# Layer norm behind the sliding-window attention: who centres, how many passes VectorE makes, and where the bias is added

## The chip, the cores and the metric

One core of one Trainium2 chip. The metric is device time in microseconds (us) of one execution. A NeuronCore has TensorE (PE in the profile; PEld is its weight load), VectorE (DVE), ScalarE (ACT), GpSimd (POOL) and SyncE (SP, which here only issues DMAs).

## The reference, cut to what matters

The program is two transformer-like blocks over 256 tokens of width 1024, all in float32. The change touches one norm of the second block, behind its sliding-window attention (index 1 of `ln_mix`):

```
for i in range(2):
    mix = ssd_shortconv_layer_mixer(x, ...) if i == 0 else sliding_window_attention(x, ...)
    x = layer_norm(ALPHA * x + mix, ln_mix_g[i], ln_mix_b[i])      # (x - mean) * rsqrt(var + 1e-5) * g + b
    x = layer_norm(ALPHA * x + (silu(x @ w_gate[i]) * (x @ w_up[i])) @ w_down[i], ln_ffn_g[i], ln_ffn_b[i])
    x = x + (p[i] @ w_ple[i]) * sigmoid(x @ w_ple_gate[i] + b_ple_gate[i])
```

So the norm's result is used twice: as the operand of the gate and up projections (11 chunks of 256 columns each), and, ALPHA times, as the residual of the next norm.

## The kernel before

**Products.** Each float32 product is made of three float32r matmuls: high part by high part, high by low, low by high. Weights come in units of at most 512 KB: SP loads a unit into one of 5 slots of `raw`, ScalarE copies it into one of 6 slots of `whi` (rounded, the high half; `high_halves(until)` does so up to a unit number), GpSimd makes `wlo = raw - whi`. SP refills a raw slot when its low half is made (`w_lo`), ScalarE refills a `whi` slot when TensorE is done with it (`w_used`). The order in which ScalarE does splits, turns and everything else is written out by hand; each engine runs its instructions in that order.

**Activations.** The operand of a product lies turned (features in partitions) in `XThi` and `XTlo` (two halves of `XT`). The stream lies in `X`, two tiles `t` of 128 tokens by 1024. To turn a half `h` (512 features) of a tile, TensorE makes four 128x128 transposes into a bank of PSUM (`turn_half`, helper line L1954), ScalarE copies the bank into `XThi` (`turn_tile`), and VectorE writes bank minus high part into `XTlo` (`turn_half`, L1129). Counters: `xh` (a half of `X` is normed), `t_pe`, `t_hi`, `t_lo`. TensorE's first feed-forward chunk `fg1_0` waits for `t_lo`: its first four rows of k want two halves of low parts (lower features of both tiles, by VectorE's order), its last four want all.

**The norm** (`layer_norm_by_tile`, name `x7`). The attention's output product is `ao0` and `ao1` (512 columns each); its last matmuls are L2675 to L2677. For each tile: VectorE adds the product to the scaled stream into a PSUM bank (`residual`, L1712), takes statistics of both halves (`bn_stats`, L1902, L1913, L1718), and their aggregate (L1719); ScalarE makes rsqrt as exp(-0.5 ln) (`layer_norm`); VectorE refines it by a Newton step (`refine_columns`, L1150 to L1156). Then VectorE makes two passes for each half: `centred`, (x - mean) * g in place (L1724), and `scaled`, times r plus b, into `X` (L1730). The rows g and b are held as `lnr[:, 0]` and `lnr[:, 1]`, broadcast over partitions.

**Around it.** TensorE's order: six `pw1_0` matmuls of tile 0 (L1982 to L1984, the product with `p`), turn of tile 0's first half, `pw1_1` of tile 0, turn of tile 0's second half, `pw1_0` and `pw1_1` of tile 1, the two turns of tile 1, feed-forward (L2016 high, L2023 low). ScalarE's: splits, root of tile 0, three splits, root of tile 1, turn of tile 0, copy of `pw1_0` to `pwt`, turn of tile 1, a split, copy of `pw1_1`. Columns such as conv weights are loaded as rows (`ROWS_B`), turned once near the start, and read by `bcol(name, j)`.

Of the kernel before, what the change touches and what calls it, by code (L numbers as in the profile page):

```python
# [211 lines left out]
ROWS_B = (("ssd_conv_w", 48), ("ssd_conv_b", 12), ("sc_conv_w", 24), ("ssd_norm_w", 8), ("b_qk", 10))  # L212
# [13 lines left out]
def build(nc, a, out):  # L226
# [8 lines left out]
    with ctx:  # L235
# [204 lines left out]
        def head_part(t, j):  # L440
# [15 lines left out]
            ln_in ln_sum ln_rs xh h_x h_g h_hi h_lo a_kd g_x g_s x_end t_half x7_t x7_f q_in act_seq dve_seq out_done""".split()  # L456
# [21 lines left out]
        def landed(name):  # L478

            return chunks[name][2]  # L480
# [118 lines left out]
        def _(act):  # L599
# [7 lines left out]
            def fn(out_, in_, func, **k):  # L607
                return nc.scalar.activation(out_, in_, func, **k)  # L608
# [42 lines left out]

            def turn_tile(name, hi, t):

                g0 = turns[name][0]
                for h in range(2):
                    g = g0 + 2 * t + h
                    act.wait_ge(S["t_pe"], g + 1)
                    bank = pm[:, g % 4, :].rearrange("p (f t) -> p f t", t=P)
                    fn(hi[:, 4 * h:4 * h + 4, t * P:(t + 1) * P], bank, ACT.Copy).then_inc(S["t_hi"], 1)
# [334 lines left out]

            def feed_forward(i):
# [4 lines left out]
                high_halves(mixed + SPLIT)  # L1000
                layer_norm(2 * i, 1)
                turn_tile(("x4", "x7")[i], XThi, 0)
                leave(f"pw{i}_0", pwt[:, 0])
                turn_tile(("x4", "x7")[i], XThi, 1)
                leave(f"pw{i}_1", pwt[:, 1])
# [91 lines left out]
        def _(v):  # L1097
# [25 lines left out]
            def turn_half(name, hi, lo, t, h):  # L1123
# [5 lines left out]
                V.tensor_tensor(lo[:, part[0], part[1]], bank, hi[:, part[0], part[1]].bitcast(F32),  # L1129
                                ALU.subtract).then_inc(S["t_lo"], 1)  # L1130
# [15 lines left out]
            def refine_columns(first, n):  # L1146
# [5 lines left out]
                for c in cols:  # L1152
                    last = V.tensor_scalar(rw[:, c], rw[:, c], -0.5, 1.5, ALU.mult, ALU.add)
# [631 lines left out]
            def feed_forward(i):  # L1785
                for c in range(DFF2 // HW):
# [9 lines left out]
                    if k:  # L1796
# [10 lines left out]
                                    ALU.subtract).then_inc(S["h_lo"], 1)  # L1807
                layer_norm(2 * i + 1, 2, (f"fd{i}_0", f"fd{i}_1"), ("x5", "x8")[i])
# [88 lines left out]
            def layer_norm_by_tile():  # L1897

                v.wait_ge(S["x7_t"], 1)
# [6 lines left out]
                summed(2, "x7", 0)  # L1906
                first_half(2, 0, "x7", 0)
                link(centred(2, 0, "x7", 0, 1))
# [860 lines left out]
```

## Time and profile before

| | us |
|---|---|
| median of 3 runs | 1247.16 (1245.83, 1247.16, 1247.21) |
| the profiled execution | 1247.44 |
| its span | 1245.6 |
| TensorE busy | 1231.2 (99%) |
| VectorE, ScalarE, GpSimd busy | 494.5, 658.1, 943.3 |
| mean granted clock of TensorE | 0.998 of full |

Busy time is the sum over one engine's instructions. TensorE's busy share says how little it waits, not how fast it works. The span is that of the instructions; 1.8 us of the execution lie around it. All times of rows below are from the start of the span.

### The profile page before, as it was taken

What the parts mean: (1) busy time and instruction counts of PE and PEld (TensorE: products, weight loads), DVE (VectorE), ACT (ScalarE), POOL (GpSimd) and SP (SyncE); (2) the same over time, 40 slices, a digit from 0 to 9 for tenths busy, and PEclk for the clock granted to TensorE, in tenths of its full rate; (3) what the DMA queues carried; (4) which work ended last, traced back from release to release, by engine and by line L of the source; (5) the groups of instructions that cost most, each with busy time, mean ns of one, the idle gap of its engine ahead of it and who ended that gap; (6) DMA issues with size and microseconds to landing.
All of it is one profiled execution on the core that took longest, in us unless ns stands there. A gap on an engine that the chain in (4) does not pass through costs nothing.

```text
span 1245.6 us, 18466 instructions
## 1 busy us (share of the span) xinstructions
PE 1231.2 (99%) x7505; PEld 1067.9 (86%) x7505; DVE 494.5 (40%) x899; ACT 658.1 (53%) x878; POOL 943.3 (76%) x409
## 2 busy tenths in 40 slices
PE   8999999999999999999999999999999999999998
PEld 7988888888888888899899888888879877888886
DVE  6635334551234310047652153342053674334025
ACT  6773656656466653345544464444445655444433
POOL 7865357838969898866589788889867657888974
PEclk9999999999999999999999999999999999999999
DMA  9754236625746666654466766666638445666651
GB/s 302 205 148 142 72 111 185 179 92 171 219 148 206 186 203 202 192 157 120 136 187 203 246 202 187 187 189 198 202 120 287 140 122 164 188 186 186 208 163 68
DMA packets 147757, 218.31 MB, mean 175 GB/s; under 512 B 9387, under 2 KB 79578, under 8 KB 147674
## 3 DMA queue, kind: packets, MB, share of 16 engines
q1 hardware_dynamic: 144282, 209.92, 55.5%
q10 hardware_dynamic: 3392, 7.23, 1.6%
q8 instruction: 59, 0.97, 0.3%
q14 instruction: 24, 0.20, 0.1%
HBM read 216.07 MB, written 1.05 MB: 174 GB/s over the span
## 4 chain that ended last, share of the span: by engine, by line
PE 93%; DVE 3%; ACT 2%; DMA 1%; POOL 1%; issue 1%; POOLq 0%; ACTq 0%; DVEq 0%
PE acc L2016 18%; PE acc L2053 12%; PE acc L2055 12%; PE acc L2054 12%; PE acc L2023 9%; PE pm L2069 6%; PE acc L2060 4%; PE acc L2062 4%; PE acc L2063 4%; PE acc L1982 1%; PE acc L1983 1%; PE acc L1984 1%; ACT whi L608 1%; PE acc L2263 1%; PE pm L1944 1%; POOL wlo L594 1%
## 5 line engine op out<-in xcount | busy, mean ns | idle before, releaser
L594 POOL TENSOR_TENSOR wlo<-raw,whi 128x1024 fp32r<-128x1024 f32 (+4 forms) x404 | 942.5, 2357 | 290.3 <-ACT whi L608 288.0
L608 ACT ACTIVATE whi<-raw 128x1024 fp32r<-128x1024 f32 (+4 forms) x404 | 410.7, 1035 | 274.8 <-PE acc L2055 134.5
L2016 PE MATMUL acc<-XT,whi 128*128 128x512 f32 x960 | 231.2, 393 | 0.0
L2016 PEld LDWEIGHTS acc<-XT,whi 128*128 128x128 f32 x960 | 177.5, 189 | 34.8 <-issue 0.2
L2023 PEld LDWEIGHTS acc<-XT,wlo 128*128 128x128 f32 x960 | 123.4, 191 | 4.8
L2023 PE MATMUL acc<-XT,wlo 128*128 128x256 f32 x960 | 124.8, 283 | 0.0
L2060 PE MATMUL acc<-XT,whi 128*128 128x256 f32 x432 | 123.2, 285 | 1.4 <-DVE XT L1118 1.4
L2053 PE MATMUL acc<-whi,XT 128*128 128x512 f32 (+4 forms) x320 | 122.7, 383 | 0.1
L2062 PE MATMUL acc<-XT,whi 128*128 128x256 f32 x432 | 122.2, 283 | 0.0
L2063 PE MATMUL acc<-XT,wlo 128*128 128x256 f32 x432 | 122.2, 283 | 0.0
L2054 PE MATMUL acc<-wlo,XT 128*128 128x512 f32 (+4 forms) x320 | 119.4, 373 | 0.0
L2055 PE MATMUL acc<-whi,XT 128*128 128x512 f32 (+4 forms) x320 | 119.4, 373 | 0.0
L2060 PEld LDWEIGHTS acc<-XT,whi 128*128 128x128 f32 x432 | 82.8, 192 | 2.3 <-issue 2.1
L2062 PEld LDWEIGHTS acc<-XT,whi 128*128 128x128 f32 x432 | 82.9, 192 | 0.1
L2063 PEld LDWEIGHTS acc<-XT,wlo 128*128 128x128 f32 x432 | 82.8, 192 | 0.0
L2053 PEld LDWEIGHTS acc<-whi,XT 128*128 128x128 f32 x320 | 60.1, 188 | 11.4 <-issue 1.3
L2055 PEld LDWEIGHTS acc<-whi,XT 128*128 128x128 f32 x320 | 60.1, 188 | 10.0
L2054 PEld LDWEIGHTS acc<-wlo,XT 128*128 128x128 f32 x320 | 60.2, 188 | 9.3 <-issue 0.2
L1712 DVE SCALAR_TENSOR_TENSOR pm<-X,acc 128x512 f32<-128x512 f32 x16 | 10.8, 692 | 108.9 <-PE acc L2055 63.7
L2053 PE MATMUL acc<-whi,Hhi 128*128 128x512 f32 x136 | 52.9, 389 | 0.0
L2054 PE MATMUL acc<-wlo,Hhi 128*128 128x512 f32 x136 | 52.9, 389 | 0.0
L2055 PE MATMUL acc<-whi,Hlo 128*128 128x512 f32 x136 | 52.9, 389 | 0.0
(423 smaller groups left out, 1952.4 us busy)
## 6 DMA issues: line engine op xcount, KB each, us to landing
raw<-in_w_in SPq DMA_DIRECT2D x68, 512.0 KB, 3.9
raw<-in_w_ff SPq DMA_DIRECT2D x64, 512.0 KB, 3.8
raw<-in_w_gate SPq DMA_DIRECT2D x44, 512.0 KB, 3.7
raw<-in_w_up SPq DMA_DIRECT2D x44, 512.0 KB, 3.8
raw<-in_w_down SPq DMA_DIRECT2D x44, 512.0 KB, 4.2
raw<-in_w_in_mix SPq DMA_DIRECT2D x36, 512.0 KB, 3.8
raw<-in_w_branch SPq DMA_DIRECT2D x16, 512.0 KB, 3.7
raw<-in_w_out_mix SPq DMA_DIRECT2D x16, 512.0 KB, 3.3
```

The costliest lines, as they stand in the source:

```text
L594: nc.gpsimd.tensor_tensor(piece(wlo, u), piece(raw, u), piece(whi, u).bitcast(F32), ALU.subtract).then_inc(S["w_lo"], 1)
L608: return nc.scalar.activation(out_, in_, func, **k)
L1944: last = T.transpose(pm[:, (g0 + g) % 4, f * TOK + t * P:f * TOK + (t + 1) * P], src[:, t, k * P:(k + 1) * P], ident)
L2016: T.matmul(acc[:, n % 2, f, :], piece(whi, u)[:, i, f * P:(f + 1) * P], XT[:, :, k, :], start=k == 0, stop=False)
L2023: last = T.matmul(acc[:, n % 2, f, 0:TOK], piece(wlo, u)[:, i, f * P:(f + 1) * P], XThi[:, k, :], start=False, stop=k == kt - 1)
L2053: T.matmul(o, hi[:, k, tok], wh, start=opens, stop=False)
L2054: T.matmul(o, hi[:, k, tok], wl, start=False, stop=False)
L2055: last = T.matmul(o, lo[:, k, tok], wh, start=False, stop=done)
L2060: T.matmul(o, wh[:, fs], hi[:, k, :], start=opens and f % 2 == 0, stop=False, skip_group_check=True)
L2062: T.matmul(o, wh[:, fs], lo[:, k, :], start=False, stop=False, skip_group_check=True)
L2063: last = T.matmul(o, wl[:, fs], hi[:, k, :], start=False, stop=done, skip_group_check=True)
L2069: return T.matmul(o, lhs, rhs, start=start, stop=stop, **k)
```

## The change

ScalarE centres the norm's rows in PSUM (`centre`: -x + mean, with the mean as a pointer bias). `refine_columns` gives the root a negative sign, and VectorE makes one pass for each half (`unbiased`: times the root, times g, into `X`). The bias b is added in two places: as a column, when the turned operand leaves PSUM (ScalarE's and VectorE's copies of a half become four 128x128 pieces each, since the column differs by 128 features), and to the stream `X` by two VectorE sums of 128x1024 inside the feed-forward, behind chunks 1 and 2. TensorE's order has `pw1_0` of tile 1 ahead of the first turn. ScalarE's order: centring of tile 0 behind its root, one split instead of three, copy of `pw1_0`, turn of tile 0's first half, root and centring of tile 1, the other turned halves, then the two splits that are left and the copy of `pw1_1`. VectorE takes tile 1's first residual ahead of tile 0's root.

```diff
@@ -209,7 +209,7 @@
           ("dn_conv_w", 48), ("norm2_g", 8), ("sg_v_norm_g", 4))
-ROWS_B = (("ssd_conv_w", 48), ("ssd_conv_b", 12), ("sc_conv_w", 24), ("ssd_norm_w", 8), ("b_qk", 10))
+ROWS_B = (("ssd_conv_w", 48), ("ssd_conv_b", 12), ("sc_conv_w", 24), ("ssd_norm_w", 8), ("b_qk", 10), ("ln_mix_b", 8))
...
@@ -649,14 +649,22 @@
+            def turn_half(name, hi, t, h, bias=None):
+                g = turns[name][0] + 2 * t + h
+                act.wait_ge(S["t_pe"], g + 1)
+                bank = pm[:, g % 4, :].rearrange("p (f t) -> p f t", t=P)
+                if bias is None:
+                    last = fn(hi[:, 4 * h:4 * h + 4, t * P:(t + 1) * P], bank, ACT.Copy)
+                else:
+                    for f in range(4):
+                        last = fn(hi[:, 4 * h + f, t * P:(t + 1) * P], bank[:, f, :], ACT.Identity, bias=bias(4 * h + f))
+                last.then_inc(S["t_hi"], 1)
             def turn_tile(name, hi, t):
-                g0 = turns[name][0]
-                for h in range(2):
-                    g = g0 + 2 * t + h
-                    act.wait_ge(S["t_pe"], g + 1)
-                    bank = pm[:, g % 4, :].rearrange("p (f t) -> p f t", t=P)
-                    fn(hi[:, 4 * h:4 * h + 4, t * P:(t + 1) * P], bank, ACT.Copy).then_inc(S["t_hi"], 1)
+                turn_half(name, hi, t, 0)
+                turn_half(name, hi, t, 1)
...
@@ -992,17 +1000,39 @@
+            def centre(t):
+                for c in range(2):
+                    x = pm[:, (turns["x7"][0] + 2 * t + c) % 4, :]
+                    fn(x, x, ACT.Identity, scale=-1.0, bias=moments[:, t, 0:1]).then_inc(S["x7_c"], 1)
             def feed_forward(i):
                 mixed = landed(("mo1b", "ao1c")[i])
                 high_halves(mixed - (APART, 3)[i] + SPLIT)
                 logs()
                 layer_norm(2 * i, 0)
-                high_halves(mixed + SPLIT)
-                layer_norm(2 * i, 1)
-                turn_tile(("x4", "x7")[i], XThi, 0)
-                leave(f"pw{i}_0", pwt[:, 0])
-                turn_tile(("x4", "x7")[i], XThi, 1)
-                leave(f"pw{i}_1", pwt[:, 1])
+                if i == 0:
+                    high_halves(mixed + SPLIT)
+                    layer_norm(0, 1)
+                    turn_tile("x4", XThi, 0)
+                    leave("pw0_0", pwt[:, 0])
+                    turn_tile("x4", XThi, 1)
+                    leave("pw0_1", pwt[:, 1])
+                else:
+                    def bias(f):
+                        return bcol("ln_mix_b", f)
+                    centre(0)
+                    high_halves(mixed - 2 + SPLIT)
+                    act.wait_ge(S["w_used"], landed("pw1_0"))
+                    fn(pwt[:, 0], accT("pw1_0"), ACT.Copy).then_inc(evac_at("pw1_0")[0], 1)
+                    turn_half("x7", XThi, 0, 0, bias)
+                    layer_norm(2, 1)
+                    centre(1)
+                    turn_half("x7", XThi, 0, 1, bias)
+                    turn_half("x7", XThi, 1, 0, bias)
+                    turn_half("x7", XThi, 1, 1, bias)
+                    high_halves(mixed + SPLIT)
+                    leave("pw1_1", pwt[:, 1])
                 for c in range(DFF2 // HW):
...
@@ -1120,14 +1150,22 @@
-            def turn_half(name, hi, lo, t, h):
+            def turn_half(name, hi, lo, t, h, bias=None):
                 g = turns[name][0] + 2 * t + h
                 v.wait_ge(S["t_hi"], g + 1)
                 bank = pm[:, g % 4, :].rearrange("p (f t) -> p f t", t=P)
                 part = slice(4 * h, 4 * h + 4), slice(t * P, (t + 1) * P)
-                V.tensor_tensor(lo[:, part[0], part[1]], bank, hi[:, part[0], part[1]].bitcast(F32),
-                                ALU.subtract).then_inc(S["t_lo"], 1)
+                if bias is None:
+                    last = V.tensor_tensor(lo[:, part[0], part[1]], bank, hi[:, part[0], part[1]].bitcast(F32),
+                                           ALU.subtract)
+                else:
+                    for f in range(4):
+                        last = V.scalar_tensor_tensor(out=lo[:, 4 * h + f, part[1]], in0=bank[:, f, :],
+                                                      scalar=bias(4 * h + f),
+                                                      in1=hi[:, 4 * h + f, part[1]].bitcast(F32),
+                                                      op0=ALU.add, op1=ALU.subtract)
+                last.then_inc(S["t_lo"], 1)
...
@@ -1143,14 +1181,14 @@
-            def refine_columns(first, n):
+            def refine_columns(first, n, sign=1.0):
                 cols = [slice(c, c + 1) for c in range(first, first + n)]
                 for c in cols:
                     last = V.tensor_scalar(rw[:, c], rv[:, c], rs[:, c], rs[:, c], ALU.mult, ALU.mult)
                 link(last)
                 for c in cols:
-                    last = V.tensor_scalar(rw[:, c], rw[:, c], -0.5, 1.5, ALU.mult, ALU.add)
+                    last = V.tensor_scalar(rw[:, c], rw[:, c], -0.5 * sign, 1.5 * sign, ALU.mult, ALU.add)
                 link(last)
...
@@ -1805,6 +1843,8 @@
                                     ALU.subtract).then_inc(S["h_lo"], 1)
+                    if i == 1 and c in (1, 2):
+                        link(V.tensor_tensor(X[:, c - 1, :], X[:, c - 1, :], lnr[:, 1, :], ALU.add))
                 layer_norm(2 * i + 1, 2, (f"fd{i}_0", f"fd{i}_1"), ("x5", "x8")[i])
...
@@ -1896,6 +1936,27 @@
+                def moments_of(t):
+                    summed(2, "x7", t)
+                    v.wait_ge(S["ln_sum"], 2 * 2 + t + 1)
+                    link(variance(rv[:, t:t + 1], moments[:, t, 1:2], 1, 1e-5))
+                def root(t):
+                    v.wait_ge(S["ln_rs"], 2 * 2 + t + 1)
+                    refine_columns(t, 1, -1.0)
+                def unbiased(t, c):
+                    cols = slice(c * W, (c + 1) * W)
+                    v.wait_ge(S["x7_c"], 2 * t + c + 1)
+                    V.scalar_tensor_tensor(out=X[:, t, cols], in0=staged("x7", t, c), scalar=rs[:, t:t + 1],
+                                           in1=lnr[:, 0, cols], op0=ALU.mult, op1=ALU.mult).then_inc(S["xh"], 1)
+                def bias(f):
+                    return bcol("ln_mix_b", f)
                 v.wait_ge(S["x7_t"], 1)
...
@@ -1903,25 +1964,26 @@
                 v.wait_ge(S["x7_f"], 2)
-                summed(2, "x7", 0)
-                first_half(2, 0, "x7", 0)
-                link(centred(2, 0, "x7", 0, 1))
-                scaled(0, "x7", 0, 1)
+                moments_of(0)
                 v.wait_ge(S["w_used"], landed("ao0c"))
                 residual(2, "ao0c", "x7", 0, 1).then_inc(evac_at("ao0c")[0], 1)
+                root(0)
+                v.wait_ge(S["ln_in"], 16 * 5 * 2)
+                unbiased(0, 0)
+                unbiased(0, 1)
                 v.wait_ge(*evac_at("ao0c"))
                 V.bn_stats(stats[:, 1, 0, :], staged("x7", 1, 0))
                 v.wait_ge(S["w_used"], landed("ao1c"))
                 residual(2, "ao1c", "x7", 1, 1).then_inc(evac_at("ao1c")[0], 1)
                 v.wait_ge(*evac_at("ao1c"))
-                summed(2, "x7", 1)
-                first_half(2, 0, "x7", 1)
-                turn_half("x7", XThi, XTlo, 0, 0)
-                link(centred(2, 0, "x7", 1, 1))
-                scaled(0, "x7", 1, 1)
-                turn_half("x7", XThi, XTlo, 1, 0)
-                turn_half("x7", XThi, XTlo, 0, 1)
-                turn_half("x7", XThi, XTlo, 1, 1)
+                moments_of(1)
+                turn_half("x7", XThi, XTlo, 0, 0, bias)
+                root(1)
+                unbiased(1, 0)
+                unbiased(1, 1)
+                turn_half("x7", XThi, XTlo, 1, 0, bias)
+                turn_half("x7", XThi, XTlo, 0, 1, bias)
+                turn_half("x7", XThi, XTlo, 1, 1, bias)
...
@@ -2691,13 +2753,13 @@
             unit_T("pw1_0", begun("pw1_0", 0), PThi, PTlo, 0)
+            enter("pw1_0")
+            unit_T("pw1_0", begun("pw1_0", 0), PThi, PTlo, 1).then_inc(S["w_used"], 1)
             turn_half("x7", 2, 0, 0)
             pe.wait_ge(S["w_lo"], begun("pw1_1", 1))
             pe.wait_ge(S["x7_f"], 2)
             unit_T("pw1_1", begun("pw1_1", 0), PThi, PTlo, 0)
             turn_half("x7", 2, 0, 1)
-            enter("pw1_0")
-            unit_T("pw1_0", begun("pw1_0", 0), PThi, PTlo, 1).then_inc(S["w_used"], 1)
             enter("pw1_1")
...
@@ -2747,7 +2809,8 @@
     arrays["rows_a"] = np.concatenate([flat(name, -1, P) for name, _ in ROWS_A])
-    arrays["rows_b"] = np.concatenate([qk_bias if name == "b_qk" else flat(name + "_2", -1, P)
+    own_rows = {"b_qk": qk_bias, "ln_mix_b": np.ascontiguousarray(inputs["ln_mix_b_2"])[1].reshape(KD, P)}
+    arrays["rows_b"] = np.concatenate([own_rows[name] if name in own_rows else flat(name + "_2", -1, P)
                                        for name, _ in ROWS_B])
     arrays["heads"] = np.concatenate([flat(name if name[0] in "df" else name + "_2", -1) for name, _ in HEADS])
     arrays["b_v"] = np.ascontiguousarray(flat("b_qkv_2", -1)[10 * P:])
```

## Rows read from the trace of the kernel before

**Rows 1.** The page's first section: engine, busy us (share) and instructions.
```profile
PE 1231.2 (99%) x7505; PEld 1067.9 (86%) x7505; DVE 494.5 (40%) x899; ACT 658.1 (53%) x878; POOL 943.3 (76%) x409
```

**Rows 2.** Waits of TensorE: line waited for, us in total, times, longest.
```profile
PE pm L1954 <- DVE X L1730: 4.3, 5, 1.6
```

**Rows 3.** Timeline of TensorE: start, us, line, operation, [idle before, releaser].
```profile
1019.68 0.39 PE L1982 MATMUL acc<-whi,PThi 128*128 128x512 f32 x1
...
1022.05 0.66 PE L1954 MATMUL pm<-ct,X 128*128 128x128 f32 x4 [0.85 <-DVE X L1730]
...
1028.93 0.66 PE L1954 MATMUL pm<-ct,X 128*128 128x128 f32 x4 [1.63 <-DVE X L1730]
1030.98 0.66 PE L1954 MATMUL pm<-ct,X 128*128 128x128 f32 x4 [1.40 <-DVE X L1730]
...
1031.67 5.49 PE L2016 MATMUL acc<-XT,whi 128*128 128x512 f32 x16
...
1038.91 3.82 PE L2016 MATMUL acc<-XT,whi 128*128 128x512 f32 x16
```

**Rows 4.** Windows: length, busy of each engine, PEclk, DMA share, GB/s.
```profile
1027.00:1031.60 4.60, 1.58 (x10) 0.84 (x8) 4.42 (x10) 2.40 (x4) 1.15 (x1) 1.00 0.77 226
...
1032.10:1035.70 3.60, 3.60 (x11) 2.80 (x10) 0.71 (x2) 2.98 (x4) 2.41 (x2) 0.53 0.02 5
```

**Rows 5.** The chain that ended last: start, us, what.
```profile
1019.70 0.77 DVE pm L1724
```

**Rows 6.** Timeline of VectorE in the norm, 1019.4 to 1033.
```profile
1020.50 0.27 DVE L1150 TENSOR_SCALAR rw<-rv,rs 128x1 f32<-128x1 f32 x1
...
1021.25 0.75 DVE L1730 SCALAR_TENSOR_TENSOR X<-pm,rs,lnr 128x512 f32<-128x512 f32 x1
1021.91 0.75 DVE L1724 SCALAR_TENSOR_TENSOR pm<-pm,moments,lnr 128x512 f32<-128x512 f32 x1
...
1024.09 0.70 DVE L1913 BATCH_NORM_STATS2 stats<-pm 128x6 f32<-128x512 f32 x1
...
1025.41 0.70 DVE L1718 BATCH_NORM_STATS2 stats<-pm 128x6 f32<-128x512 f32 x1
...
1026.39 0.15 DVE L1138 TENSOR_SCALAR rv<-moments 128x1 f32<-128x1 f32 x1
...
1030.84 1.28 DVE L1129 TENSOR_TENSOR XT<-pm,XT 128x512 fp32r<-128x512 f32 x2
```

**Rows 7.** ScalarE's groups by shape: line, operation, shapes, busy us, mean ns.
```profile
L608 ACT ACTIVATE pm<-pm 128x512 f32<-128x512 f32 x24 | 14.0, 582 | 12.3 <-DVE pm L1659 11.8
...
L608 ACT ACTIVATE XT<-pm,colA 128x256 fp32r<-128x256 f32 x16 | 6.4, 483 | 1.9 <-PE pm L1944 1.6 <-PE pm L2095 0.3
...
L608 ACT ACTIVATE dn<-X,rs 128x512 f32<-128x512 f32 x1 | 0.7, 722 | 0.1
...
L608 ACT ACTIVATE bmt<-pm 128x256 f32<-128x256 f32 x1 | 0.4, 366 | 0.0
```

**Rows 8.** Timeline of ScalarE in the norm: the splits behind tile 0's root.
```profile
1019.95 2.94 ACT L608 ACTIVATE whi<-raw 128x1024 fp32r<-128x1024 f32 x3
```

**Rows 9.** VectorE: two timelines (pieces) and a group by shape (SBUF sum).
```profile
601.43 2.16 DVE L1659 SCALAR_TENSOR_TENSOR pm<-pm,acs,ct 128x128 f32<-128x128 f32 x8
...
14.26 1.66 DVE L1118 SCALAR_TENSOR_TENSOR XT<-pm,colA,XT 128x256 fp32r<-128x256 f32 x4 [0.80 <-ACT XT L608]
...
L1331 DVE TENSOR_TENSOR dn<-dn 128x1024 f32<-128x1024 f32 x1 | 1.2, 1219 | 0.0
```

**Rows 10.** Timeline of ScalarE in the attention: four Identity activations, pointer bias.
```profile
986.34 1.58 ACT L608 ACTIVATE aqT<-acc,colB 128x256 f32<-128x256 f32 x4
```

**Rows 11.** Timeline of GpSimd through the norm.
```profile
1021.07 7.08 POOL L594 TENSOR_TENSOR wlo<-raw,whi 128x1024 fp32r<-128x1024 f32 x3 [2.48 <-ACT whi L608]
1033.29 4.73 POOL L594 TENSOR_TENSOR wlo<-raw,whi 128x1024 fp32r<-128x1024 f32 x2 [5.14 <-ACT whi L608]
```

**Rows 12.** Timeline of VectorE in the feed-forward: the copy that opens a chunk.
```profile
1050.24 0.69 DVE L1792 COPY sg<-acc 128x512 f32<-128x512 f32 x1 [2.05 <-PE acc L2023]
```

More of the change, by code:

```diff
@@ L455, in build @@
             s_acc s_eac s_xe s_st s_stc s_yo s_yod b_row b_e0 b_e b_m b_y b_yd y_ss y_n c_out c_hi c_lo
-            ln_in ln_sum ln_rs xh h_x h_g h_hi h_lo a_kd g_x g_s x_end t_half x7_t x7_f q_in act_seq dve_seq out_done""".split()
+            ln_in ln_sum ln_rs xh h_x h_g h_hi h_lo a_kd g_x g_s x_end t_half x7_t x7_f x7_c q_in act_seq dve_seq out_done""".split()
         S = {n: sem(n) for n in names}
```

## The prediction

> **What bounds the kernel now.** The page comes first: TensorE is busy for 99% of the span [rows 1]. So a change pays only where TensorE waits, or where its clock falls. Next the waits by engine: over the whole run TensorE's longest wait is for rows that VectorE scaled in a norm, 4.3 us in 5 pieces [rows 2]. The timeline places most of it behind the attention. TensorE does six `pw1_0` matmuls of tile 0 from 1019.68 to 1021.20, idles 0.85 us for the first scaled half, later 1.63 us (from 1027.30) and 1.40 us (from 1029.58) for tile 1's halves, and starts the feed-forward at 1031.67 [rows 3]. That is 3.88 us idle. The first sixteen feed-forward matmuls then take 5.49 us, the next chunk's sixteen 3.82 [rows 3]: 1.67 us more. The windows show why: the granted clock is a mean 0.53 from 1032.1 to 1035.7, so it was at the lower of its two levels (1.2 GHz against 2.4) for nearly all of that stretch; in the 4.60 us before the feed-forward, at 1.00, TensorE had been busy for 1.58 [rows 4]. All that there is to win here is 3.9 + 1.7 = 5.6 us, 0.45% of the run. The chain of waits runs through VectorE in this stage, centring among it [rows 5].
>
> **The change, part by part.** I lay the new order out in span time; each start follows from a row's start-to-start distance.
>
> TensorE: the second six matmuls of `pw1_0` move ahead of the first turn. Six took 1.5 us [rows 3], so they run from about 1021.1 to 1022.6 and cover the wait of 0.85 us. Their bank needs tile 1's `ao0c` residual, see next.
>
> VectorE, tile 0: `centred` is gone, and tile 1's residual takes its slot at 1019.70 [rows 5]. The root goes 0.75 us from its first step to the scaling [rows 6], so the scaling starts at about 1021.05, not 1021.25: the gain is small, because residual and centring cost nearly the same. The second half is scaled 0.66 us later, at 1021.71, with no centring between. Then, at the old distances: statistics 0.66 later (1022.37), residual and statistics in 1.32 (1023.69), aggregate and variance in 0.98 (1024.67, over at 1024.82) [rows 6]. Before, that variance began at 1026.39: 1.7 us saved.
>
> ScalarE takes over the centring, 128x512 in PSUM with a pointer bias. No row is that operation: without a pointer it takes 582 ns in PSUM, with a pointer scale and from SBUF 722 ns [rows 7]. I take 0.68, starts 0.56 apart: the PSUM row is nearest, plus 0.1 us for the pointer (the 128x256 rows without and with one, 366 and 483 ns) [rows 7]. The exponential is over by 1019.95 [rows 8], so tile 0's halves are centred by 1020.63 and 1021.19, ahead of their use by 0.4 and 0.5 us. Then one weight split to 1022.15 (three take 2.94 us) [rows 8], the `pwt` copy when TensorE is through, 1022.6 to 1023.64 (as wide as a split), and the first turned half.
>
> The hand-off of a turned half is now four 128x128 pieces on each engine, for the bias. VectorE: eight such pieces with a pointer take 2.16 us [rows 9], so starts 0.26 apart and 1.13 us for four; now it is 0.64 (two in 1.28) [rows 6]. ScalarE: the 128x256 form runs four in 1.58 us, 483 ns each, so starts 0.365 apart; 256 columns less are 0.216 us less (582 against 366 ns), 128 less 0.108 [rows 7, 10]: starts 0.26 apart, 1.16 us for four; now it is 0.60. Ends: as cheap as a whole half (0.64 and 0.60) or as dear as the 128x256 pieces (1.66 and 1.58) [rows 9, 10]; I stay with the 128x128 row. The Trainium skill's page "ScalarE: Activation LUTs", section "What ACT_TABLE_LOAD costs", says that a pointer operand adds about 93 ns and that activations back to back overlap by as much; by its figures four pieces would be about 1.27 us, an estimate, and the start of the feed-forward 0.1 us later than in my sum. No activation table comes with Identity: the queries run four of them among exponentials [rows 10] and no load stands before them.
>
> So ScalarE has the first half turned at 1024.70, just as the aggregate is there (1024.64). Logarithm and exponential follow at 1024.73 and 1025.06; tile 1's halves are centred by 1025.85 and 1026.41, the next half turned by 1027.48. VectorE: four pieces 1024.86 to 1025.99, then the root, scaling from 1026.65 and 1027.31, over at 1027.40 and 1028.06. TensorE, 0.85 us of idle less in front, is through with `pw1_1` at 1026.4 instead of 1027.30, waits 1.05 us, turns from 1027.45 and 1028.11, and ends at 1028.75, where it was 1031.64. The old last wait is gone.
>
> A new one takes its place. The feed-forward's first matmuls want the lower rows of both tiles, high and low parts. Before, VectorE's pair of turned halves from 1030.84 [rows 6] had them ready as the last turn ended. Now ScalarE starts tile 1's first half at 1028.14 (1.16 us), VectorE follows at 1029.34 (1.13 us): ready at 1030.47. TensorE idles 1.75 us and starts at 1030.50 instead of 1031.67. The upper rows are due at 1032.5; at the lower clock the first eight matmuls last beyond 1033, at full clock until 1032.3, a wait of 0.2 us. **Sum: 1.17 us gained**; 3.88 us of idle become about 2.8.
>
> The clock: before, TensorE was idle for 3.0 of the 4.4 us ahead of the feed-forward; now for 2.8 of 4.1, the same share. It fell there, so I let it fall again at the same 1.67 us.
>
> What I cost at nothing, and its cover. The up-projection's two splits, done by 1022.9 before [rows 8], now stand behind the turned halves on ScalarE, to about 1030.2. GpSimd, idle from 1028.15 to 1033.29 [rows 11], makes their low halves from 1031.3 to 1036.0 (three took 7.08); TensorE wants the first of them at 1039.9 at the earliest, some 4 us of cover. The weight loads on SP's queue that these free come some 8 us later, for units that TensorE reaches after 1047. Without the cover each low half costs up to 2.4 us. The two 128x1024 bias sums on VectorE (1.22 us each by the SBUF row [rows 9]) go where it idles 2.05 us before the next chunk's copy [rows 12]; uncovered they would be 2.4 us. Eight more rows in a table loaded at the start, and eight columns in its copy: nothing measurable.
>
> **The rivals.**
> *The clock does not fall.* For it: the new cluster of gaps is 0.3 us shorter in all, and one of the three runs is 1.3 us shorter than the others, as if it had been spared. Against it: the same idle share as before, and a longest gap of 1.75 us where it was 1.63. It gives 1.17 + 1.67 - 0.2 = 2.6 us: 1244.5. The Trainium skill's page "TensorE: Matmul & The Clock Gate", section "Why this matters for your kernels", asks for no idle gap over about 3 us between bursts; by that rule no gap here, old or new, slows the clock. The trace of before disagrees: gaps of 1.63 and 1.40 us around one turn were enough.
> *The pieces are dear (slower).* If four pieces cost what four 128x256 pieces do, the chain grows by 0.53 (VectorE ahead of the root), 0.42 and 0.53 us (the last hand-off): the feed-forward starts at 1031.98, 0.3 us later than before: 1247.5. It decides once these three hand-offs, 3.4 us in my sum, pass 4.6. For it: each piece has its own fixed part. Against it: VectorE's 128x128 row.
> *ScalarE holds it back, no gain.* It runs in order, and tile 1's logarithm stands behind the `pwt` copy and the first turned half. Anything that delays these (the six matmuls, a split that waits for its buffer) delays the root; my margin is under 0.1 us, and 1.2 us of delay leave nothing: 1247.2. Against it: both predecessors have a slot of their own length in the rows.
>
> **How the numbers follow.** The profiled execution took 1247.44 us, 1245.6 of them the span; the median shown is 1247.16, 0.3 lower, and I count from it: 1247.16 - 1.17 = 1246.0. Chances: forecast 0.62, clock that does not fall 0.24, dear pieces 0.08, ScalarE late 0.06. The range takes in the clock case and the dear pieces with some room: 1244.2 to 1247.6. What can be told from no change is 0.2%, 2.5 us, so down to 1244.7. The forecast is inside it. The clock case just passes it, in perhaps two of three of its outcomes, and pieces as cheap as a whole half (1.46 us less) add 0.05: faster 0.21. Slower by that much needs a lost cover: 0.04. Same: 0.75.
>
> **What the changed profile would show.** Right: no wait before the first turn; tile 1's aggregate at 1024.4; the last turn over at 1028.8; then 1.7 us of idle that VectorE's pieces end; the feed-forward from 1030.5, at a clock near 0.5 for a few us. Wrong: ScalarE's pieces more than 0.3 us apart, tile 1's logarithm well after its aggregate, TensorE waiting for a low half of the weights, or full clock after the stage.

## The result: 0.6% slower, with the norm itself faster

| | before | after |
|---|---|---|
| median of 6 runs each, us | 1246.87 | 1254.54 (1253.51 to 1254.82) |
| ratio, 95% interval | | 1.0061 (1.0051 to 1.0072) |
| the profiled execution, us | 1247.44 | 1254.82 |
| its span, us | 1245.6 | 1252.8 |

The forecast was 1246.0 us, with a range of 1244.2 to 1247.6. The measured time lies 7 us above the range.

The page of the changed kernel, busy us and instructions by engine, and three of its groups (busy us, mean ns of one, idle before):

```profile
PE 1240.3 (99%) x7505; PEld 1068.2 (85%) x7505; DVE 494.9 (40%) x909; ACT 662.4 (53%) x894; POOL 944.3 (75%) x409
...
L2078 PE MATMUL acc<-XT,whi 128*128 128x512 f32 x960 | 231.2, 393 | 1.8 <-DVE XT L1164 1.8
...
L2116 PE MATMUL acc<-wlo,XT 128*128 128x512 f32 (+4 forms) x320 | 119.4, 373 | 0.0
...
L2115 PE MATMUL acc<-whi,Hhi 128*128 128x512 f32 x136 | 53.8, 396 | 0.0
```

The same two kinds of group in the kernel before:

```profile
L2016 PE MATMUL acc<-XT,whi 128*128 128x512 f32 x960 | 231.2, 393 | 0.0
...
L2054 PE MATMUL acc<-wlo,XT 128*128 128x512 f32 (+4 forms) x320 | 119.4, 373 | 0.0
...
L2053 PE MATMUL acc<-whi,Hhi 128*128 128x512 f32 x136 | 52.9, 389 | 0.0
```

TensorE does the same 7505 matmuls as in [rows 1] and is busy 9.1 us longer. Groups that read `XT` are as they were, groups that read `Hhi` take 396 ns instead of 389. In the timeline this shows as a slower pace, and it is there already half a millisecond ahead of the changed norm. First the kernel before, then the changed one (start us, us):

```profile
499.73 0.39 PE L2053 MATMUL acc<-whi,FFhi 128*128 128x512 f32 x1
499.95 0.39 PE L2054 MATMUL acc<-wlo,FFhi 128*128 128x512 f32 x1
500.18 0.39 PE L2055 MATMUL acc<-whi,FFlo 128*128 128x512 f32 x1
...
501.31 0.39 PE L2054 MATMUL acc<-wlo,FFhi 128*128 128x512 f32 x1
```

```profile
499.78 0.40 PE L2115 MATMUL acc<-whi,FFhi 128*128 128x512 f32 x1
500.01 0.40 PE L2116 MATMUL acc<-wlo,FFhi 128*128 128x512 f32 x1
500.25 0.40 PE L2117 MATMUL acc<-whi,FFlo 128*128 128x512 f32 x1
...
501.41 0.40 PE L2116 MATMUL acc<-wlo,FFhi 128*128 128x512 f32 x1
```

From the first start shown to the last, seven steps further, it is 1.58 us before (0.226 a step) and 1.63 us after (0.233), with no wait in either. Taken over the whole trace (distances of 400 ns and more, which are waits, left out), the mean distance from one matmul's start to the next one's grows from 226.8 to 229 ns to 233 to 235 ns in the 128x512 groups whose stationary operand (the first of the two that a matmul call names, its weights; the second is the moving one) is `Hhi`, `Hlo`, `FFhi`, `FFlo`, `BYhi`, `BYlo`, `BRhi` or `BRlo` (`BRhi`'s high group, with its stalls, from 234.6 to 239.5). These are 1,295 matmuls, and the sum over them is 8.0 us. Less the 1.0 us that the norm gains (below) this leaves 7.0, and the two spans differ by 7.2.

Next the norm behind the attention, on TensorE, from the timeline of the changed kernel. It starts 6.5 us late there, at 1026.22 where [rows 3] have 1019.68:

```profile
1026.22 0.40 PE L2044 MATMUL acc<-whi,PThi 128*128 128x512 f32 x1
...
1029.02 0.60 PE L2016 MATMUL pm<-ct,X 128*128 128x128 f32 x4
...
1030.85 0.60 PE L2016 MATMUL pm<-ct,X 128*128 128x128 f32 x4
...
1033.96 1.32 PE L2016 MATMUL pm<-ct,X 128*128 128x128 f32 x8 [1.11 <-DVE X L1954]
1037.10 5.50 PE L2078 MATMUL acc<-XT,whi 128*128 128x512 f32 x16 [1.82 <-DVE XT L1164]
```

The clock there, to be held against [rows 4] (stretch, its length, busy us of each engine, then PEclk):

```profile
1032.60:1037.10 4.50, 1.56 (x10) 0.87 (x9) 3.13 (x10) 3.72 (x14) 0.00 (x0) 1.00 0.31 106
...
1037.50:1040.90 3.40, 3.40 (x11) 2.61 (x10) 1.52 (x6) 3.40 (x5) 3.05 (x2) 0.57 0.00 0
```

The wait in front of the first turn is gone, three waits of 3.88 us have become two of 2.93, and the clock falls again: the first sixteen feed-forward matmuls take 5.50 us, as in [rows 3]. The distance from VectorE's first residual to the feed-forward is 1037.10 - 1022.92 = 14.18 us after, 1031.67 - 1016.47 = 15.20 before: 1.02 us gained. The residual of the kernel before, then the starts on the other engines in the changed one:

```profile
1016.47 0.70 DVE L1712 SCALAR_TENSOR_TENSOR pm<-X,acc 128x512 f32<-128x512 f32 x1 [1.38 <-PE acc L2677]
```

```profile
1022.92 0.69 DVE L1750 SCALAR_TENSOR_TENSOR pm<-X,acc 128x512 f32<-128x512 f32 x1 [1.39 <-PE acc L2739]
...
1027.48 1.41 DVE L1954 SCALAR_TENSOR_TENSOR X<-pm,rs,lnr 128x512 f32<-128x512 f32 x2
...
1031.10 0.15 DVE L1176 TENSOR_SCALAR rv<-moments 128x1 f32<-128x1 f32 x1
1031.37 1.13 DVE L1164 SCALAR_TENSOR_TENSOR XT<-pm,colB,XT 128x128 fp32r<-128x128 f32 x4
...
1033.15 1.41 DVE L1954 SCALAR_TENSOR_TENSOR X<-pm,rs,lnr 128x512 f32<-128x512 f32 x2
```

```profile
1026.39 1.22 ACT L608 ACTIVATE pm<-pm,moments 128x512 f32<-128x512 f32 x2
...
1030.14 1.13 ACT L608 ACTIVATE XT<-pm,colB 128x128 fp32r<-128x128 f32 x4
...
1034.65 2.17 ACT L608 ACTIVATE XT<-pm,colB 128x128 fp32r<-128x128 f32 x8 [0.78 <-PE pm L2016]
```

### The profile page after: what moved, and what is told of

Its sections match the earlier page's. It is cut to its first block, busy times and chain, and to the rows that moved or that the text cites. A ratio compares the mean times of both kernels' runs of the same rounds, so it can differ in the third digit from the quotient of the medians.

```text
span 1252.8 us, 18492 instructions
## 1 busy us (share of the span) xinstructions
PE 1240.3 (99%) x7505; PEld 1068.2 (85%) x7505; DVE 494.9 (40%) x909; ACT 662.4 (53%) x894; POOL 944.3 (75%) x409
## 4 chain that ended last, share of the span: by engine, by line
PE 95%; DVE 2%; ACT 1%; issue 0%; POOL 0%; DMA 0%; POOLq 0%; ACTq 0%; DVEq 0%
PE acc L2078 18%; PE acc L2115 13%; PE acc L2117 12%; PE acc L2116 12%; PE acc L2085 9%; PE pm L2131 6%; PE acc L2122 4%; PE acc L2124 4%; PE acc L2125 4%; PE acc L2044 1%; PE acc L2046 1%; PE acc L2045 1%; PE pm L2006 1%; PE acc L2325 1%; PE acc L2327 1%; PE acc L2326 1%
```

## What differs far from the norm: a theory

Eight more rows of `ROWS_B` make `colB` eight columns wider. Tiles lie in SBUF in the order in which the program allocates them, so each tile allocated behind `colB` starts 32 bytes higher in every partition. By the addresses in the built program `raw`, `whi` (from byte 21632), `wlo` (46208), `X` and `XT` (78976) lie ahead of it and stay; `BRhi` and `FFhi` move from 107136 to 107168, and `Hhi`, `BYhi`, `AThi`, `PThi` with them. In the kernel before, all of these begin 128 bytes past a multiple of 512.

The theory is that the pace of a matmul depends on where its two operands lie in SBUF. It has two rivals: some part of the new order, or its extra instructions, slows TensorE; or the eight rows alone cost the time, by what is loaded and copied.

## The experiments

A tile named `apart`, which nothing reads or writes, lies between `XT` and the tiles behind it: 32 columns in both kernels. Its width is the knob. All runs of "before, shifted" have the unchanged instructions of the kernel before.

**1. The changed kernel, its tiles back at the old addresses.**

```diff
-        sb("apart", [P, 32])
+        sb("apart", [P, 24])
```

> The changed kernel with an unused pad of 32 columns cut to 24, so that every tile behind the pad has its old address again (the eight new columns had pushed it 32 bytes up); nothing else differs. Theory A (address): the three-matmul products whose stationary operand lies behind the pad start 227 ns apart again instead of 233, some 1,300 of them, so about 8.3 us come back: 1246.2 us, and the stage of the norm still gains its 1.0 us. Theory B (the norm or the order of the engines costs it): nothing changes, 1254.5 us. Theory C (half of it is elsewhere): about 1250.

Measured: 1246.76 us (11 runs) beside 1247.31 (15 runs), ratio 0.9999 (0.9991 to 1.0008). TensorE's page and groups in it:

```profile
PE 1231.9 (99%) x7505; PEld 1068.4 (86%) x7505; DVE 495.2 (40%) x909; ACT 662.4 (53%) x894; POOL 943.9 (76%) x409
...
L2115 PE MATMUL acc<-whi,Hhi 128*128 128x512 f32 x136 | 52.9, 389 | 0.0
```

The whole loss is gone with 32 bytes. The order, the pieces and the bias sums cost nothing that the timing can tell, and they gain nothing that it can tell either. The norm in this run, on TensorE:

```profile
1022.34 0.60 PE L2016 MATMUL pm<-ct,X 128*128 128x128 f32 x4
...
1027.37 1.32 PE L2016 MATMUL pm<-ct,X 128*128 128x128 f32 x8 [1.20 <-DVE X L1954]
1030.51 5.49 PE L2078 MATMUL acc<-XT,whi 128*128 128x512 f32 x16 [1.82 <-DVE XT L1164]
```

This is the kernel that the prediction worked on: it had the last turns from 1027.45 and the feed-forward at 1030.50. That about 1 us gained in this stage doesn't show in the median has a likely reason in the clock, argued here and not shown. The mean granted clock of an execution was 0.997 or 0.998 in all eleven runs of this kernel. Among the fifteen runs of the kernel before that were taken beside it, three have 1.00 (1245.57 to 1246.15 us) and ten 0.999 (1246.84 to 1247.89): the old order keeps its clock now and then (see experiment 5), and then it is the faster one.

**2. The kernel before, shifted.** Nothing changes but the width of `apart`:

```diff
-        sb("apart", [P, 32])
+        sb("apart", [P, 40])    # +32 bytes; 36: +16; 48: +64; 64: +128; 160: +512
```

> The kernel before with the unused pad at 40 columns instead of 32: everything behind it 32 bytes higher, no instruction changed. Theory A: 8 us slower, 1255 us, with starts 233 ns apart in products with FFhi, Hhi, BRhi, BYhi as stationary operand and 227 in those with XT. Theory B: 1246.9.

> The kernel before with the pad at 48 columns: the same tiles 64 bytes higher. If what matters is where the operand lies within 64 bytes: 1246.9, starts 227 ns apart. If it must lie on 128 bytes (as all did before): about 1255. If any shift costs by its size: more than 1255.

> The kernel before with the pad at 36 columns: the same tiles 16 bytes higher. If any start off a 64-byte line costs the same (an operand then spans one line more): about 1255. If a line of 16 bytes is enough: 1246.9. If the cost follows the offset: about 1251.

> The kernel before with the pad at 64 columns: every tile behind it 128 bytes higher. Shifts of 16, 32 and 64 bytes all cost some 8.5 us, and all operands stood on multiples of 128 bytes. If the start within 128 bytes is what matters: 1247, starts 227 ns apart. If these tiles must keep their distance from others, or lie on 256 bytes or more: 1256.

> The kernel before with the pad enlarged so that all tiles behind it start 512 bytes higher. If the pattern repeats every 512 bytes: 1247 us, 227 ns. If it repeats only over longer distances or not at all: about 1255 us, 233 ns in the groups whose operand moved.

| bytes | 16 | 32 | 64 | 128 | 512 |
|---|---|---|---|---|---|
| us | 1255.87 | 1255.64 | 1256.46 | 1254.81 | 1247.15 |
| ratio | 1.0069 | 1.0071 | 1.0074 | 1.0059 | 1.0001 |
| interval | 1.0051 to 1.0088 | 1.0055 to 1.0086 | 1.0056 to 1.0093 | 1.0041 to 1.0078 | 0.9991 to 1.0011 |
| start to start, stationary `Hhi`, moving `whi`, ns | 234.3 | 234.5 | 234.3 | 233.4 | 228.1 |

So 32 bytes in the kernel before cost what the change cost, and any of the four steps from 16 to 128 costs nearly the same. Of the five, only 512 bytes are free. A start at a multiple of 128 bytes isn't enough: with 128 the pace is nearly as slow as with 16.

**3. Which tile?** First `XT` 32 bytes higher, with `apart` eight columns narrower so that all behind `apart` stays. The tiles between the two, `ct` and the small columns, move along; of the operands of the three-matmul products `XT` alone does.

```diff
+        sb("pad_xt", [P, 8])
         XT = sb("XT", [P, 2, KD, TOK], F32R)
...
-        sb("apart", [P, 32])
+        sb("apart", [P, 24])
```

> The kernel before with XT alone 32 bytes higher (8 columns of pad ahead of it, 8 fewer behind). If a stationary operand off its 128 bytes costs 6 ns for each matmul of 512 columns: the 720 matmuls of L2053 to L2055 with XT and 512 columns, 120 of L1982 to L1984 and 48 of L2263 to L2265 start 233 ns apart, 5.6 us slower, 1252.5; the feed-forward's matmuls, where XT moves and the weights stand still, keep 228 ns. If the moving operand counts as well, these (960, 240) slow down too: up to 1259.

Then both weight tiles 32 bytes higher, with 96 more bytes behind them, so that all behind them is 128 higher (from the weights to every other operand it is 96 bytes more):

```diff
+        sb("pad_w", [P, 8])
         whi = sb("whi", [P, SPLIT, UK, BANK], F32R)
         wlo = sb("wlo", [P, SPLIT, UK, BANK], F32R)
+        sb("pad_x", [P, 24])
```

> The kernel before with whi and wlo 32 bytes higher, all behind them 128 bytes higher. Here the moving operand of the three-matmul products is off, and the stationary operand of the feed-forward's (1920) and of the F products. If only the stationary side counts: products with FFhi, Hhi, XT stationary keep 227 ns, and the feed-forward's 960 matmuls of 512 columns slow by 6 ns, 6 us, 1253, with up to 6 more for those of 256. If the moving side counts: the 2,200 three-matmul products slow down, 13 us, 1260. If neither: 1247.

And every tile 32 bytes higher, by a pad of eight columns ahead of the first, which keeps all distances:

> The kernel before with a padding tile of 32 bytes a partition ahead of the first tile, so that every tile in SBUF starts 32 bytes higher and all distances between tiles are kept. Theory that the distance between the stationary and the moving operand of a matmul sets the pace: nothing changes, 1247 us, 128x512 matmuls 227 ns from start to start. Rival, the absolute start address decides: all 512-column groups at 233 ns as in the run with shifted weights, 1260 us or more.

Measured: 1249.16 us (ratio 1.0016, 1.0006 to 1.0026) for `XT` alone; 1265.97 (1.0149, 1.0130 to 1.0167) for the weights; 1247.38 (1.0002, 0.9992 to 1.0013) for all. Mean distance from start to start in ns, 512 and 256 columns, the stationary operand first (distances over 300 ns, for 256 columns over 160, left out as waits):

| operands | before | `XT` +32 | weights (96) | all +32 |
|---|---|---|---|---|
| `whi`, `XT` 512 | 228.4 | 233.3 | 233.3 | 228.4 |
| `XT`, `whi` 512 | 227.8 | 233.3 | 234.2 | 228.0 |
| `Hhi`, `whi` 512 | 226.7 | 227.1 | 234.1 | 226.6 |
| `whi`, `XT` 256 | 119.8 | 117.1 | 119.6 | 119.8 |
| `wlo`, `XT` 256 | 119.6 | 116.9 | 120.2 | 119.6 |

The last column decides between an absolute address and a distance: with every tile 32 bytes on, nothing changes. What counts is how far the two operands of a matmul, stationary and moving, lie apart. In this table no group changes by more than 0.4 ns unless its distance did. The second column has a surprise: at the new distance 512-column matmuls lose 5 to 5.5 ns and 256-column ones gain 2.7. Both expectations for the single shifts missed the time. `XT` alone was put at 1252.5 or up to 1259, and the gain of the 256 columns was in neither; the weights were put at 1253 or 1260, by the place of one operand or the other, while in fact every 512-column group is slow at once. The page of the run with `XT` alone has it in the mean durations (393 and 283 ns in the kernel before):

```profile
L2017 PE MATMUL acc<-XT,whi 128*128 128x512 f32 x960 | 235.6, 397 | 0.0
...
L2024 PE MATMUL acc<-XT,wlo 128*128 128x256 f32 x960 | 122.0, 279 | 0.0
```

**4. `XT` 256 bytes higher**, all behind `apart` 512.

```diff
+        sb("pad_xt", [P, 64])
...
-        sb("apart", [P, 32])
+        sb("apart", [P, 96])
```

> The kernel before with XT 256 bytes higher and all tiles behind it 512 bytes higher, so that only the groups that read XT have an operand at another place in a stretch of 512 bytes. If every step but 0 in 512 costs the same as 32 bytes did: 1249 us, the 512-column groups with XT about 4 ns slower, the 256-column ones about 3 ns faster. If 256 bytes is as good as 0: 1247 us and no group differs. A third outcome, 512-column groups kept and 256-column ones faster, would give about 1240 us.

Measured: 1246.23 us, 0.9993 (0.9983 to 1.0003); the groups with `XT` at 228.4 (stationary `whi`) and 228.0 ns (moving `whi`) for 512 columns, and at 119.8 and 119.6 ns for 256. The distance works modulo 256 bytes as far as these runs go: 0, 256 and 512 are equal for 512 columns, 16, 32, 64, 96 and 128 are slow.

**5. The two waits that are left, and the clock.** In the realigned kernel, eleven filler matmuls of 512 columns on `PThi` (four ahead of tile 1's turns, seven behind) keep TensorE busy where it would idle; they write a bank that has been read.

```diff
+            def fill(count):
+                for _ in range(count):
+                    T.matmul(acc[:, chunks["pw1_0"][0] % 2, 0, :], PThi[:, 0, 0:P],
+                             PThi[:].rearrange("p a b -> p (a b)"), start=True, stop=True)
+            pe.wait_ge(*evac_at("pw1_0"))
+            fill(4)
...
+            fill(7)
```

> e1_after_realigned with matmuls of no use in TensorE's two waits of the norm: four of 512 columns ahead of tile 1's turns (0.9 of 1.2 us), seven behind them (1.6 of 1.8 us), into a bank that the feed-forward opens anew. If the clock falls for want of matmuls in this stretch: it stays at full, the first sixteen feed-forward matmuls take 3.9 us and not 5.5, 1.4 to 1.7 us off: 1245.2 against 1246.8, and the runs lie closer together. If the fall has nothing to do with it: 1246.8 or, where the fillers delay a turn, up to 1247.5.

Measured: 1246.25 us (11 runs), ratio 0.9991 (0.9982 to 1.0000).

```profile
1022.84 0.60 PE L2016 MATMUL pm<-ct,X 128*128 128x128 f32 x4
...
1026.51 1.07 PE L2769 MATMUL acc<-PThi 128*128 128x512 f32 x4
1027.87 1.32 PE L2016 MATMUL pm<-ct,X 128*128 128x128 f32 x8 [0.29 <-DVE X L1954]
1028.94 1.86 PE L2769 MATMUL acc<-PThi 128*128 128x512 f32 x7
1031.01 4.13 PE L2078 MATMUL acc<-XT,whi 128*128 128x512 f32 x16 [0.21 <-DVE XT L1164]
1034.98 2.08 PE L2085 MATMUL acc<-XT,wlo 128*128 128x256 f32 x16
```

The first sixteen take 4.13 us instead of 5.49, because the clock, at 0.52 over a stretch of 3.4 us in experiment 1, is now 1.00:

```profile
1031.00:1035.20 4.20, 4.18 (x18) 3.23 (x19) 1.94 (x8) 4.20 (x5) 3.43 (x2) 1.00 0.00 0
```

From the first turn to the next chunk's high part it is 14.06 us instead of 15.41. The median moved by less, 0.5 us (it was expected at 1245.2), and the two intervals overlap. The traced execution had lost 0.50 us ahead of the first turn and loses another 0.55 us behind this stage; why stays open. That the filler keeps the clock shows in the runs too: the mean granted clock was 0.999 or 1.00 in all eleven, where experiment 1 had 0.997 or 0.998.

The old order doesn't lose its clock every time. With the same waits in front, the first sixteen took 5.49 us in the kernel before and 3.89 in the run with 32 bytes of experiment 2, at a clock of 1.00:

```profile
1035.66 0.66 PE L1954 MATMUL pm<-ct,X 128*128 128x128 f32 x4 [1.59 <-DVE X L1730]
1037.71 0.66 PE L1954 MATMUL pm<-ct,X 128*128 128x128 f32 x4 [1.39 <-DVE X L1730]
1038.40 3.89 PE L2016 MATMUL acc<-XT,whi 128*128 128x512 f32 x16
```

It was spared also in the traces with every tile 32 bytes higher (3.89), with `XT` 256 higher (3.87) and with the weights shifted (3.98), and not in those with 16, 64 and 128 bytes (5.51, 5.47, 6.40), with `XT` alone (5.40) and, in part, with 512 bytes (4.85).

**6. A finer wait** on top of experiment 5: the first feed-forward rows of k wait only for the two pieces of `XTlo` that they read.

```diff
+                        if f == 1 and t == 1 and h == 0:
+                            last.then_inc(S["x7_p"], 1)
...
-            fill(7)
+            fill(5)
```

> The changed kernel with the old addresses and filler matmuls, and besides that the first feed-forward rows wait only for the pieces of XT that they read, with two filler matmuls fewer. Theory: the feed-forward part starts about 0.5 us earlier and the time is 1245.7 us, 0.5 below the run without it (1246.25). Rival: the later rows wait for the rest of the pieces and nothing is gained, 1246.2.

Measured: 1245.78 us (11 runs), ratio to the kernel before 0.9986 (0.9977 to 0.9995), with the interval just clear of 1. But the trace sides with the rival of the expectation:

```profile
1023.17 0.60 PE L2018 MATMUL pm<-ct,X 128*128 128x128 f32 x4
...
1030.82 2.07 PE L2080 MATMUL acc<-XT,whi 128*128 128x512 f32 x8
1033.41 2.06 PE L2080 MATMUL acc<-XT,whi 128*128 128x512 f32 x8 [0.51 <-DVE XT L1164]
1035.31 2.08 PE L2087 MATMUL acc<-XT,wlo 128*128 128x256 f32 x16
```

The feed-forward starts 0.52 us earlier, counted from the first turn (7.65 against 8.17 us), and then waits 0.51 us for the second piece group. The low part begins 12.14 us after the first turn in both. VectorE's last pieces end the stage, and the runs of the two kernels overlap almost wholly (1245.05 to 1246.88 and 1244.92 to 1246.56 us); 0.5 us between the medians can't be put down to this edit.

**7. The distance put to use.** 256 bytes of padding behind each of the six slots of `wlo`, and the low halves of weights that 256-column matmuls read lie 224 bytes into their slot (`XT` is then 32 bytes above them modulo 256); those that 512-column matmuls read lie at its start. Modulo 256 bytes no other operand moves against another.

```diff
-        wlo = sb("wlo", [P, SPLIT, UK, BANK], F32R)
+        wloP = sb("wlo", [P, SPLIT, UK * BANK + 64], F32R)
+        wlo = wloP[:, :, 0:UK * BANK].rearrange("p s (u b) -> p s u b", b=BANK)
...
+            if buf is wlo and unit_mode[u] in "FB":
+                slot = wloP[:, u % SPLIT, SHIFT:SHIFT + UK * BANK].rearrange("p (u b) -> p u b", b=BANK)
```

with `SHIFT` 56 (224 bytes), and in a second kernel 8 (32 bytes, the distance with the other sign).

> The run before this one (changed kernel, old addresses, filler, finer wait) with 256 bytes of padding behind each slot of wlo, and the low halves of units used by 256-column matmuls 224 bytes into their slot, so that XT lies 32 bytes above them modulo 256 (as in the run with XT alone shifted), while every 512-column matmul keeps its distance. If the distance between the two operands of a matmul sets its pace: the some 1450 wlo,XT 256-column matmuls go from 119.6 to 117.0 ns, all 512-column groups stay at 227 to 228, and the time is 3.8 us below 1245.8, 1242.0. Rival, the gain of the 256-column ones came from something else that moved with XT (its absolute place, or the distance to the high weights): no change, 1245.8.

> The same with the low halves 32 bytes into their slot, so that XT lies 32 bytes below them modulo 256. If only whether the distance is a multiple of 256 counts: as the run with 224 bytes, 1242.0 us if that one gains. If the sign or the size counts: another pace than 117.0 ns in the wlo,XT 256-column group, 119.6 or worse.

Measured: 1240.60 us (1240.44 to 1240.99, 5 runs), ratio 0.9944 (0.9931 to 0.9958), and 1243.89 us (7 runs), 0.9971 (0.9960 to 0.9981). The first:

```profile
PE 1226.2 (99%) x7514; PEld 1062.4 (86%) x7514; DVE 493.7 (40%) x909; ACT 662.5 (53%) x894; POOL 943.9 (76%) x409
...
L2096 PE MATMUL acc<-XT,wlo 128*128 128x256 f32 x960 | 122.1, 279 | 0.0
L2135 PE MATMUL acc<-XT,whi 128*128 128x256 f32 x432 | 121.7, 282 | 0.0
L2136 PE MATMUL acc<-XT,wlo 128*128 128x256 f32 x432 | 120.8, 280 | 0.0
L2127 PE MATMUL acc<-wlo,Hhi 128*128 128x512 f32 x136 | 52.9, 389 | 0.0
```

The `wlo`, `XT` 256 group goes from 119.6 to 117.0 ns, as expected (1,446 matmuls, 3.75 us), and the 512-column ones stay at 227 to 229. But the `whi`, `XT` 256 group, whose own distance didn't change, goes from 119.8 to 117.7 too: 2.05 us more, over 969. In the products where both are read in turn, a `wlo` matmul stands next to each of them, and the trace tells its two neighbours apart: a `whi` matmul that follows one goes from 119.9 to 117.0 ns, one that stands ahead of one from 119.7 to 118.4. So the operands of the matmuls around it count as well, not only the pair of one matmul. The two gains are 5.8 us, less 0.5 for `whi`, `XT` 512 (228.4 to 228.9 ns): that is why the time fell by 5.2 us where 3.8 were expected. With the other sign `wlo`, `XT` 256 is at 118.5 ns, `whi`, `XT` 256 at 117.9 and `whi`, `XT` 512 at 230.0: the sign or the size counts, though 118.5 isn't the "119.6 or worse" that was expected.

Two more numbers of these traces bear on the reach of the effect. In the feed-forward, sixteen `whi`, `XT` 512 matmuls stand in a row between 256-column ones of `wlo`. The last of such a row (62 of them), whose own operands kept their distance, goes from 226.7 ns to 235.0 with 224 bytes and to 234.9 with 32: only the next matmul's weights lie elsewhere. And with 32 bytes the second to the ninth of a row go from 229.3 to 231.1 ns, though their own operands and both neighbours' are as before; from the tenth to the fifteenth they stay at 226.7 and 226.8. So something that went before still counts some matmuls later; what it is, no run shows. The kernel with 224 bytes beats both that the case began with.

## Why the prediction was wrong

The step that failed is one line of the prediction: "Eight more rows in a table loaded at the start, and eight columns in its copy: nothing measurable." The load and the copy do cost nothing that can be told (experiment 1 keeps them, at 0.9999). What cost 8.0 us is where these columns push the tiles behind them: a term that the working put at nothing because it priced edits only where they execute. Experiments 1 and 2 show it from both ends: the change without the shift is at 0.9999 and the shift without the change at 1.0071. "Slower by that much needs a lost cover" named the wrong kind of cause for a loss, so its chance of 0.04 was too low.

The steps about the norm, read against the profile (starts of the changed kernel less 6.45 us, by which its first residual is late):

- The scaling of tile 0 was put at 1021.05 and tile 1's variance at 1024.67. They are at 1027.48 - 6.45 = 1021.03 and 1031.10 - 6.45 = 1024.65. Right.
- ScalarE's centring was put at 0.68 us each with starts 0.56 apart, so 1.24 for two: 1.22. Right. The value near the PSUM row was the right one.
- Four pieces were put at 1.13 us on VectorE and 1.16 on ScalarE: 1.13 and 1.13 to 1.14. Right, so "the pieces are dear" is refuted. The estimate of 1.27 us worked out from the Trainium skill's page "ScalarE: Activation LUTs", section "What ACT_TABLE_LOAD costs", was too high.
- ScalarE doesn't hold tile 1's root back: its logarithm starts at 1031.13, 0.03 us after the variance's start.
- The new wait was put at 1.75 us: 1.82. The feed-forward at 1030.50: 1030.51 in experiment 1, 1037.10 - 6.45 = 1030.65 in the changed kernel, where the matmuls on `PThi` are slower too. The gain in this stage, put at 1.17 us, was 1.02.
- The clock fell again, as forecast, and at the same price (5.50 us for sixteen). But the ten traces of the old order show that this varies from one execution to the next: six lost it (one of them in part) and four kept it. The prediction had the fall as a certainty in its sum and the other outcome as a rival for the whole; neither holds for a median alone. The Trainium skill's page "TensorE: Matmul & The Clock Gate", section "Why this matters for your kernels", asks for no gap over about 3 us; here the longest is 1.82 us in the new order and 1.63 in the old, so these traces go against it wherever the clock fell.
- The covers held: no wait of TensorE for a low half of the weights in this stage, and the two bias sums of 1.22 us ran at 1064.68 and 1075.82 inside the feed-forward without one.

So for the stage that it looked at, the prediction's layout is that of experiment 1, within 0.1 us. The time isn't shown to be: 1246.0 was forecast, 0.9991 of the kernel before, and experiment 1 measured 1246.76 with a ratio of 0.9999 (0.9991 to 1.0008), which holds the forecast at its very edge and no gain at all near its middle.

## What to carry to other kernels

An edit that adds a few columns to a tile moves all that are allocated behind it. Before a change is credited or blamed, compare the mean duration of TensorE's largest groups far from the edit: if the same instructions have changed pace, look at the start addresses first. Keep the distances between the operands of 256-column and of 512-column matmuls under your own control with padding tiles, and time a few: here the placement was worth more (0.6 to 0.7% lost in experiment 2, 0.4% won in experiment 7) than the reordering of a whole stage.

## What the runs showed of the hardware

- 128x512 matmuls in float32r, back to back, start every 227 to 228 ns when the stationary and the moving operand start a multiple of 256 bytes apart in the partition (0, 256, 512 seen) and every 233 to 235 ns at 16, 32, 64, 96 or 128 bytes. The absolute address doesn't count in the one run that tells: all tiles 32 bytes on gives 227 to 228 again.
- 128x256 matmuls are fastest at another distance: 119.6 to 119.8 ns at a multiple of 256, 116.9 to 117.1 with the moving tile 32 bytes above the weights, 118.5 with it 32 below, 119.6 to 120.2 at 96. A matmul's pace hangs on the operands of others near it too (119.8 to 117.7 ns for a group whose own distance stayed, 226.7 to 235.0 ns for matmuls where only the weights that follow moved).
- The cause inside the chip stays open. That the load of the next stationary operand and the running matmul's reads of its moving operand meet somewhere would fit the last number, where only the next weights lie elsewhere; it doesn't by itself explain why 256 columns are fastest at another distance, or why matmuls some places further on are slower. No run varies what the other engines read and write in SBUF meanwhile, so their part in it is open too. The Trainium skill's page "TensorE: Matmul & The Clock Gate", section "Step-by-step: what each phase is for", says that loading the next tile's weights takes no SBUF read bandwidth from the running matmul. If a meeting of the two is the cause, the measured 5 to 8 ns a matmul speak against it.
- Waits of 1.6 and 1.4 us around one turn dropped the granted clock to its lower level in some executions and not in others of the same instructions (5.49 and 3.89 us for the same sixteen matmuls). Filler matmuls in the two waits of the new order kept it at 1.00 in the traced execution (4.13 us), and at a mean of 0.999 or 1.00 in all eleven runs.
